# A layer of RWKV-7 mixing, chunk MLP and conv MLP: the modulation columns of each pair computed by VectorE inside the scan instead of by TensorE in the inversion

## What is computed

```python
mod = jax.nn.silu(c) @ w_mod + b_mod              # (2048) @ (2048, 12288)
sh1, sc1, gt1, sh2, sc2, gt2 = jnp.split(mod[:, None, :], N_MOD, axis=-1)
h = rmsnorm(x, g_pre1) * (1.0 + sc1) + sh1
p = h @ w_in                                      # then rwkv_mixer and chunk_mlp on p
x = x + gt1 * rmsnorm(mix, g_post1)
h2 = rmsnorm(x, g_pre2) * (1.0 + sc2) + sh2
x = x + gt2 * rmsnorm(conv_glu_ffn(h2, w_up, conv_ffn, w_down, grid=True), g_post2)
```

## Time and profile before

| | us |
|---|---|
| median of 3 runs | 3207.3 (3206.77 to 3211.29) |
| the profiled execution | 3207.55 |
| its span, first to last instruction | 3205.8 |
| mean granted TensorE clock in the span | 0.964 |
| a pass of the pair loop, 562.18 to 666.15 and 666.15 to 767.65 | 103.97 and 101.50 |

### The profile page before, as it was taken

One profiled execution on the slowest core, in us unless ns is written; L12 is line 12 of the kernel. 1 busy time (PEld: TensorE's weight loads), 2 busy tenths in 40 slices (PEclk: granted clock), 3 DMA queues, 4 the chain that ended last, 5 costly groups with the idle time before them and its releaser, 6 DMA issues.

```text
span 3205.8 us, 70945 instructions
## 1 busy us (share of the span) xinstructions
PE 2982.5 (93%) x28320; PEld 2250.8 (70%) x28320; DVE 1745.8 (54%) x3292; ACT 951.8 (30%) x1635; POOL 434.1 (14%) x580
## 2 busy tenths in 40 slices
PE   5899999998999999999999899999999999999997
PEld 1245555555555555555556569999989999999997
DVE  1135545564456545564456345444348888886444
ACT  1122212222122222222122143333344444443333
POOL 0001100111111110111011102000002333331000
PEclk8899999999999999999999999999999999999999
DMA  7512222121222222122222244555444555554553
GB/s 313 240 71 98 79 73 89 61 100 61 87 79 74 87 74 82 59 100 74 74 80 87 108 165 152 182 183 183 165 169 144 181 181 181 181 182 162 178 180 134
DMA packets 66106, 412.81 MB, mean 129 GB/s; under 512 B 8176, under 2 KB 10864, under 8 KB 25328
## 3 DMA queue, kind: packets, MB, share of 16 engines
q1 hardware_dynamic: 65136, 407.51, 35.4%
q0 software_dynamic: 768, 2.10, 0.2%
HBM read 405.38 MB, written 4.19 MB: 128 GB/s over the span
## 4 chain that ended last, share of the span: by engine, by line
PE 82%; DVE 9%; issue 4%; DMA 2%; ACT 2%; POOL 0%; SPq 0%; DVEq 0%; ACTq 0%; POOLq 0%; PEldq 0%
PE PB L651 16%; PE Q L899 6%; PE Q L900 6%; PE Q L904 6%; PE PB L899 4%; PE PB L900 4%; PE PB L904 4%; PE CH L904 3%; PE CH L900 3%; PE CH L899 3%; DVE arena L1402 2%; PE Q L767 2%; PE Q L784 2%; DMA ring<-w_mod_dram 2%; PE PB L636 2%
## 5 line engine op out<-in xcount | busy, mean ns | idle before, releaser
L651 PE MATMUL PB<-hT,ring 128*128 128x512 f32 (+1 forms) x1536 | 686.6, 556 | 5.4 <-PEq L640 5.4
L1585 DVE TENSOR_TENSOR w_lo_r<-ring,w_hi_r 128x1536 fp32r<-128x1536 f32 (+3 forms) x178 | 387.5, 2177 | 268.9 <-ACT w_hi_r L1194 268.9
L1194 ACT ACTIVATE w_hi_r<-ring 128x2048 fp32r<-128x2048 f32 (+2 forms) x178 | 325.7, 1830 | 452.4 <-PE Q L904 211.4
L651 PEld LDWEIGHTS PB<-hT,ring 128*128 128x128 f32 x1536 | 251.9, 189 | 139.6 <-issue 95.9
L900 PE MATMUL PB<-hT_r,w_hi_r 128*128 128x256 f32 x832 | 204.6, 285 | 0.0
L1745 DVE TENSOR_TENSOR w_lo_r<-ring,w_hi_r 128x1408 fp32r<-128x1408 f32 x62 | 101.2, 1633 | 148.0 <-ACT w_hi_r L1308 148.0
L899 PE MATMUL PB<-hT_r,w_hi_r 128*128 128x256 f32 x704 | 175.7, 289 | 4.7 <-DVE hT_r L1672 4.7
L899 PE MATMUL Q<-ff_hi_r,w_hi_r 128*128 128x256 f32 x704 | 175.6, 288 | 1.8 <-ACT w_hi_r L1308 1.8
L900 PE MATMUL Q<-ff_lo_r,w_hi_r 128*128 128x256 f32 x704 | 172.9, 284 | 0.0
L899 PE MATMUL CH<-hT_r,w_hi_r 128*128 128x256 f32 x704 | 170.9, 283 | 0.0
L900 PE MATMUL CH<-hT_r,w_hi_r 128*128 128x256 f32 x704 | 170.9, 283 | 0.0
(11 more groups left out here) (262 smaller groups left out, 6028.3 us busy)
## 6 DMA issues: line engine op xcount, KB each, us to landing
ring<-w_mod_dram SPq DMA_DIRECT2D x96, 1024.0 KB, 5.0
ring<-w_up_dram SPq DMA_DIRECT2D x88, 1024.0 KB, 4.8
ring<-w_rkv_dram SPq DMA_DIRECT2D x48, 1024.0 KB, 4.9
ring<-w_down_dram SPq DMA_DIRECT2D x64, 704.0 KB, 4.0
ring<-w_ga_dram SPq DMA_DIRECT2D x16, 1024.0 KB, 4.8
ring<-w_gb_dram SPq DMA_DIRECT2D x16, 1024.0 KB, 4.8
ring<-w_pa_dram SPq DMA_DIRECT2D x16, 1024.0 KB, 4.8
ring<-w_out_dram SPq DMA_DIRECT2D x16, 1024.0 KB, 4.8
```

Source lines behind the costliest of these rows:

```text
L651: last = mm(PB[slot % 2][:, 0:cols], tile(n, kt), hT[:, kt, 0:cols], start=(kt == 0), stop=(kt == KT - 1))
L1194: f(w_hi_r[:, r % 2, 0:n], ring[:, r, 0:n], ACT.Copy).then_inc(hi_rdy, 1)
L1585: tt(w_lo_r[:, r, 0:n], ring[:, r, 0:n], as_f32(w_hi_r[:, r % 2, 0:n]), ALU.subtract).then_inc(lo_rdy, 1)
```

## The change

The four tiles of `w_mod` are no longer multiplied by TensorE. `mod_acc` is a 128 x 512 accumulator in SBUF, which takes over the buffer `TL` (used by the inversion's start). VectorE's new `mod_product(i, k)` multiplies the 128 x 512 block k of the pair (tile k // 4, quarter k % 4) by the column `csilp[:, k, 0:1]`, one value a partition, and adds it to `mod_acc`: a `ts` for k = 0 and an `stt` for k = 1 to 15, each behind a wait for the one before (`mac_rdy`). The first of a tile waits for the load. After the last of a tile, VectorE releases the region.

In the pairs 0 to 14 the products 2s and 2s+1 stand at the end of scan step s. In the last pair, where no inputs are prepared, they stand in the inversion's levels 0 to 3, two after the mask and two after the updates.

TensorE adds up the 128 partitions in the tail, ahead of the mean: four matmuls with `mod_acc` as weights and two columns of ones, after a wait for the 16th product. ScalarE's copy falls away, as do the `mod_cp` waits. VectorE adds `b_mod` after the deviation, for the latent column alone. A wait for `mod_rdy` before the scores of the next pair keeps TensorE from overwriting the sums.

```diff
+        mod_acc = TL.rearrange("p c t -> p (c t)")
@@ TensorE, body
                 pe.wait_ge(rs_rdy, i + 1)
+                pe.wait_ge(mod_rdy, i + 9)
...
                         last.then_inc(zl_ps, 1)
-                    if lv:
-                        region(3, "pair", lv - 1, i, 4)
-                        mod_tile(3, CH[1], lv - 1)
...
-                pe.wait_ge(mod_cp, i + 10)
                 for s in range(NCH):
...
-                    if s == 0:
-                        mod_sums(Q[3])
...
                     project(i + 2, 1, 0, 3)
+                pe.wait_ge(mac_rdy, i * 16 + 16)
+                for n in range(4):
+                    last = mm(Q[3][:, 2 * n:2 * n + 2], mod_acc[:, n * P:(n + 1) * P], ones[:, 0:2], start=True, stop=True)
+                last.then_inc(mod_sum, 1)
                 pe.wait_ge(ysum_rdy, i + 1)
@@ ScalarE, body
-                product(3, "pair", 3, i, 4)
-                f(mod_sb, CH[1][:, :].rearrange("p (a b) -> p a b", b=P), ACT.Copy).then_inc(mod_cp, 1)
@@ VectorE
+            def mod_product(i, k):
+                n, q = k // 4, k % 4
+                w, c = ring[:, 3, q * 4 * P:(q + 1) * 4 * P], csilp[:, k, 0:1]
+                if q == 0:
+                    dve.wait_ge(loaded[3], i * 64 + 16 * (loads_before("pair")[3] + n + 1))
+                if k == 0:
+                    dve.wait_ge(zl_rdy, i * (LEVELS - 1) + 1)
+                    ts(mod_acc, w, c, None, ALU.mult).then_inc(mac_rdy, 1)
+                else:
+                    dve.wait_ge(mac_rdy, i * 16 + k)
+                    stt(mod_acc, w, c, mod_acc, ALU.mult, ALU.add).then_inc(mac_rdy, 1)
+                if q == 3:
+                    dve.wait_ge(mac_rdy, i * 16 + k + 1)
+                    dve.sem_inc(used[3], 1)
@@ VectorE, body, levels
                     if more >= 1:
                         inputs(i + 1, 2 * lv)
+                    elif lv < 4:
+                        mod_product(i, 4 * lv)
+                        mod_product(i, 4 * lv + 1)
...
                     if more >= 1:
                         inputs(i + 1, 2 * lv + 1)
+                    elif lv < 4:
+                        mod_product(i, 4 * lv + 2)
+                        mod_product(i, 4 * lv + 3)
@@ VectorE, body, scan
-                    if s == 1:
-                        dve.wait_ge(mod_sum, i + 10)
-                        mod_out(Q[3][:, 0:8], i * 4 + 32).then_inc(mod_rdy, 1)
...
+                    if more >= 1:
+                        mod_product(i, 2 * s)
+                        mod_product(i, 2 * s + 1)
                     if more >= 1 and s == NCH - 2:
                         outer(i + 1, 2, par_v)
@@ VectorE, body, tail
                 stt(ra, Q[0][:, 0:T], -1.0 / HEAD, ra, ALU.mult, ALU.add).then_inc(dev_rdy, 1)
+                dve.wait_ge(mod_sum, i + 10)
+                tt(modT[:, bass.ds(i * 4 + 32, 4), 0], Q[3][:, 0:8].rearrange("p (a b) -> p a b", b=2)[:, :, 0],
+                   bmod[:, bass.ds(i * 4 + 32, 4)], ALU.add).then_inc(mod_rdy, 1)
```

More of the change, by code:

```diff
@@ L252, in layer_kernel @@
         mod_sum = sem("mod_sums_done")
+        mac_rdy = sem("mod_products_added")
         mod_rdy = sem("mod_rows_ready")
```

## The result

The changed kernel takes **3268.2 us** (median of 4 runs, 3259.7 to 3281.5) where the kernel before takes 3207.0: a ratio of 1.019, interval 1.016 to 1.023. The forecast was 3292, its range 3225 to 3340. The execution profiled took 3269.6 us around a span of 3267.9.

A forecast was written before the change was run, and what follows sets the result against it. TensorE, busy 2982.5 of 3205.8 us, was taken as the bound where the chain runs over it. Loop passes +71 (14 x +5.1), pair 14 +7 and last pair +7 give +85 on 3207.3: 3292 us, range 3225 to 3340.

The forecast's parts named there:

- three tiles off TensorE: Inversion levels: three w_mod tiles on TensorE's part of the chain, 1.00 us each, removed; gain 3.0 us a pass.
- products in the scan: Scan steps: VectorE's two products of 0.75 us fit in each ordinary step with 0.36 us to spare; cost 0.
- round trips of the loads: Scan steps 2, 4 and 6: the single region's next tile arrives late, by 1.8, 0.9 and 1.4 us; 4.1 a pass.
- tail: End of a pass: the four sums (1.0 us) ahead of the mean delay later matmuls by 0.4 us.
- clock: Longer TensorE waits at s = 0, 2 and 6 bring 1.5 more half-clock stretches a pass, 3.6 us; bounds 0 and 7.5.
- loads of tile 0 and w_rkv, moved: SyncE's queue: both loads move about 1 us later, but are wanted tens of us later; cost nothing.
- rival of slow products: Rival: products in the scan take 1.3 to 1.4 us each, +8.5 us a pass, some 3420 us; chance 0.08.
- The fourth tile and the sums: Scan start: removing these gains nothing; TensorE's wait for VectorE's copy grows from 0.5 to 2.5 us.
- Pair 15: Last pair, products in the inversion: three loads cost 7 us, 3 come back, 3 for the clock; +7 us.
- Tiles that give nothing: Rival: the inversion's 3.0 us turn into waits for VectorE; +42 us, 3334 us; chance 0.08.
- clock that stays up: Rival: loads cost as forecast but no new half-clock stretch comes; +31 us, 3238 us; chance 0.17.
- The rival of 3168 us (the loads hide): Rival: next tile within 3.1 us of release, VectorE never waits; -2.4 us a pass; chance 0.06 faster, 0.06 about equal.

The follow-up runs named there:

- e6: e2 with unread matmuls in the loop's scans, two in step 0 and one in step 7; 3178.2 us, ratio 0.991.
- e8: e6 with tile 0's loads moved behind those of lora_w and w_r (region 1) on SyncE's queue, out of the tail; 3157.1 us, ratio 0.985.
- e7: The changed kernel without the four matmuls that sum over the partitions in the tail; 3263.2 us, ratio 1.017.
- e3: The changed kernel with unread matmuls in TensorE's waits, two in scan steps 0 and 7, one in step 3; 3241.4 us, ratio 1.010.
- e9: The changed kernel with only the load of a pair's tile 0 placed behind lora_w's; 3274.1 us, ratio 1.022.
- e11: The kernel before with only w_k's load moved behind lora_w's, out of the tail; 3207.8 us, ratio 1.0006.
- e2: The changed kernel with each w_mod tile loaded as two halves of 512 KB, each released when read; 3185.5 us, ratio 0.992.
- e1: The changed kernel with one load of w_mod a pair instead of four, all 16 products reading that tile; 3193.0 us, ratio 0.995.
- e4: The changed kernel without the products and the w_mod loads in the pairs, the sums kept; 3195.3 us, ratio 0.995.
- e5: e4 with two unread matmuls in step 0 of each scan of the loop; 3140.4 us, ratio 0.980.
- e12: e8 without the unread matmuls; 3176.1 us, ratio 0.991.

## Why the prediction came out as it did

The direction and the mechanism were right, the forecast was 24 us too high, and one term of the sum was missing. A loop pass, forecast and measured:

| term | forecast | measured | from |
|---|---|---|---|
| three tiles off TensorE | -3.0 | -3.0 | levels 6.06 for 7.05 us |
| products in the scan | 0 | 0 | 29.16 us in e6, e8 |
| round trips of the loads | +4.1 | +3.4 | 1.5 (s = 2), 0.65 (s = 4), 1.28 (s = 6) |
| tail | +0.4 | about 0 | e7 |
| clock | +3.6 | +2.3 | after less e3 |
| loads of tile 0 and w_rkv, moved | 0 | +1.5 | the stop, mean of e3 and of before (4.65, 3.13) |
| sum | +5.1 | +4.2 | +4.37 by the starts of the passes |

The clock and the stop, 3.8 us together, are split here by e3, which takes the half clock out first. Taken the other way round the stop is worth nothing in this kernel, since half clock hides it: e9 moves the load and takes 3274.1 us beside 3268.2. The terms for loads, tail and clock were 2.4 us a pass too high together and the missing one is 1.5 by this split, so that the sum came within 1 us a pass is in part luck.

**The product** was taken at 0.75 us and is 0.752 in the median (ns min/median/max over 240):

```profile
L1465 DVE SCALAR_TENSOR_TENSOR arena<-ring,csilp,arena x240: 740/752/979, 307.3 to 1892.2; 128x512 f32<-128x512 f32 x120
```

The rival of slow products falls. By the Trainium skill's "Vector Engine (DVE) Microarchitecture Reference", "Points that are easy to get wrong", both sources in SBUF and fp32 would halve the throughput; the prediction's estimate for that was 1.4 us, and no product of this kernel shows it.

**The round trips** were worked out step by step and each was somewhat too long: 1.8, 0.9, 1.4 forecast. At s = 2 the load was issued at 1595.02 and VectorE could start at 1599.82, 5.03 us after its last product had ended (1594.79) and not 5.2; the rest is in the copy, seen by TensorE 0.28 us behind the products' end and not 0.4.

**The fourth tile and the sums** gained nothing at s = 0, as said: the wait there is 2.48 us (2.5 forecast). The sums cost TensorE 0.95 us at the place foreseen, 1.71 in the nine tails at half clock, and e7 shows no price for them beyond the spread.

**The clock** was right in kind: the waits at s = 0 and at the scan's end each start stretches at half clock in most passes. The amount was close: 1.5 stretches of 6.8 us more a pass were forecast, 10.2 us, and it is 10.0 us more, in 33 stretches of 3.4 to 13.7 us instead of 15. The price was too high. The 2.5 us for a stretch were read where TensorE sets the pace, and the slower of those two passes has 5.3 us more of half clock than the other, not 6.8. Nor was it one pass of 14 in which the wait of 1.65 us brought half clock, but two (the first and the fourth); after, it is four. Here much of the half clock falls in the tail, where TensorE waits for others and then for the stop, which half clock hides (4.85 us at full clock, 1.48 at half).

**The step that failed** is the sentence "The loads of the pair's first tile and of w_rkv move behind the later releases on SyncE's queue by about 1 us; they are wanted tens of us later, so nothing." That their data are wanted tens of us later holds. That both move by about 1 us does not. Against L835 of s = 7 (1269.38 before, L832 at 884.07 after) w_k's load moves from 1.7 us behind it (1271.11) to 3.2 us behind it (887.23), but tile 0's moves from 5.9 us ahead of it (1263.48) to 2.6 us behind it (886.62), out of the scan into the tail. And I asked only who wants their data: issued within 0.6 us of each other, what the two delay is the jump. By the stops it is 1.5 us a pass at full clock; e8 against e6 has it at 21 us in all, half clock included, and e9 at nothing in the changed kernel.

**Pair 14** was +7 and is +6.4. **Pair 15** was +7 and is +0.6. Its three loads are as slow as said (the chain):

```profile
1865.21 4.88 DMA ring<-w_mod_dram
1874.61 4.86 DMA ring<-w_mod_dram
1883.99 4.76 DMA ring<-w_mod_dram
```

Its inversion takes 7.6 us more. But then the 5.8 us between inversion and scan, most of them the wait of 4.69 us for w_v, shrink to 0.3, and the scan is 1.5 us shorter: 7.0 come back where 3 were counted. The reason given, that the region is free earlier, stands; its worth was set too low. And the passes begin 6.4 us earlier, since the stretches of half clock ahead of the loop fell otherwise (47.8 us of it instead of 54.6); no term stood for that. It is scatter and not the change: e11, whose code is that of before up to there, begins its passes at 249.6 us as well.

**The rivals.** Tiles that give nothing fall by the levels of 6.06 us. The clock that stays up was put at 3238 us; e3, which is that case made by hand, takes 3241, with two errors in it that cancel in part: the loads and the tail cost 1.1 us a pass less than said, the stop 1.5 more.

The sum with what was measured: 61 + 6 + 1 - 6 = 62 us of span. The rival of 3168 us (the loads hide) named the right condition. e2 meets it, a half tile landing in 3.6 us and wanted a whole step later, and is 21.5 us faster than before rather than 39, the stop and the clock taking the difference.

## What to carry over

Moving work from the engine that bounds a kernel to an idle one frees what the chain ran over it, here 3.0 us a pass, but the buffer changes hands with it: look at how long the new reader holds the buffer and when the next load is wanted, and cut the load so that the round trip fits; here two halves turned +2% into -0.8%. For each load that moves in a queue ask not only who wants its data, but what else goes through the DMA engines at its new place; a loop's jump does. Price a stretch of half clock by the engine's slack where it falls, and try a few unread matmuls in the wait before believing such a price.

## What the runs showed of the hardware

- The jump of a loop costs TensorE 2.8 to 3.4 us of standing still at full clock, in this kernel 13 times; a packet of instructions starts on the DMA engines just behind TensorE's end, and the pass starts 2.5 to 3.0 us after the packet's start. Behind two weight transfers of 1 MB the stop is 4.4 to 5.0 us (e1, e3). In e8 it is 4.9 us twice with no such transfer near, but with two packets there. Without a jump the last tail of the loop, which runs on into pair 14's own code, takes 9.5 us before where the others take 12.5.
- Waits of 2.5 us at s = 0 brought half clock behind them (e4, all 14 passes); with the wait filled up to 0.76 us it stayed full (e5).
- What half clock costs differs by where it falls. In e5, passes with 5.7 to 5.9 us of it take 99.1 to 99.3 us and passes without any 96.7 to 96.9. In the changed kernel 10.5 us more of it a pass than in e3 cost 2.3 us.
- Three unread matmuls a pass made the kernel with half tiles and a late tile 0 19 us faster (e8 against e12).
